# The context tiles' first layer half moved from a stage of its own into the 32 experts before it

## The reference

```python
def expert_block(args):                       # first block, per expert
    xb, e = args
    gt = xb @ w_gate[e] + b_gate[e]
    up = xb @ w_up[e] + b_up[e]
    gt = jnp.minimum(gt, SWIGLU_LIMIT)
    up = jnp.clip(up, -SWIGLU_LIMIT, SWIGLU_LIMIT)
    hdn = gt * jax.nn.sigmoid(SWIGLU_ALPHA * gt) * (up + 1.0)
    return hdn @ w_down[e] + b_down[e]
...
def chunk_mlp(h, n_chunks, w_in, norm_g, norm_b, w_s, b_s, w_out):
    z = jax.nn.gelu(h @ w_in)
    u, v = jnp.split(z, 2, axis=-1)
    v = layer_norm_2(v, norm_g, norm_b)
    vb = v.reshape(bsz, n_chunks, CHUNK, A_HEADS, A_GROUP)
    s = jnp.einsum('hpq,bnqhc->bnphc', w_s, vb) + b_s.T[None, None, :, :, None]
    return (u * s.reshape(bsz, t, A_WIDTH)) @ w_out
...
def one_block(xb):                            # peer_ffn, 8 heads, 128 + 128 sub-keys
    q = (xb @ w_q).reshape(PEER_BLOCK, PEER_HEADS, 2, PEER_HALF)
    s = jnp.einsum('thpd,pkd->thpk', q, sub_keys).astype(jnp.float32)
    # top 16 of either half, top 16 of the 256 sums, softmax
    act = jax.nn.gelu(jnp.einsum('thkd,td->thk', u_tab[idx], xb)) * wts
    return jnp.einsum('thk,thkd->td', act, v_tab[idx])
...
# second block, layer 0: x are the 256 latent tokens (the first block's output), ctx 256 given ones
h_lat = x * (1.0 + s1) + sh1
mix_lat = chunk_mlp(h_lat, lat_chunks, *prm)
mix_ctx = chunk_mlp(ctx * (1.0 + s1c) + sh1c, ctx_chunks, *prm)
x = layer_norm_2(DN_ALPHA * x + g1 * mix_lat, ln_g[i, 0], ln_b[i, 0])
ffn_lat = peer_ffn(x * (1.0 + s2) + sh2, ...)
ctx = layer_norm_2(DN_ALPHA * ctx + g1c * mix_ctx, ln_g[i, 0], ln_b[i, 0])
ffn_ctx = peer_ffn(ctx * (1.0 + s2c) + sh2c, ...)
```

## Time and profile before

| what | us |
|---|---|
| three runs | 3847.1, 3851.69, 3853.88 (median 3851.69) |
| the profiled execution | 3846.67 |
| its span, from the first to the last instruction | 3844.9 |
| PE busy | 3362.8 (87%) |
| DVE busy | 1772.8 (46%) |
| ACT busy | 1112.3 (29%) |
| POOL busy | 855.5 (22%) |
| mean rate of the DMA engines | 359 GB/s |

### The profile page before, as it was taken

How to read it: one execution, slowest core, us unless ns; L and a number is a source line. 1 busy time by engine, 2 the same in 40 slices (tenths; PEclk the granted TensorE clock), 3 DMA queues, 4 the chain that set the end, 5 groups by cost and what they waited for, 6 DMA issues and landing times. The chain is left out here.

```text
span 3844.9 us, 36626 instructions
## 1 busy us (share of the span) xinstructions
PE 3362.8 (87%) x11836; PEld 1520.8 (40%) x11836; DVE 1772.8 (46%) x4114; ACT 1112.3 (29%) x2981; POOL 855.5 (22%) x796
## 2 busy tenths in 40 slices
PE   8988999999999988788979779898887987877876
PEld 7635444444444435333335324343323543322322
DVE  0152211111111133576676686668753256767665
ACT  0141011111111111343343344544333213434333
POOL 0010000000000000334444344344440004444442
PEclk9999799999999989899999999999999988999999
DMA  6496699999999942999999999999996109999998
GB/s 277 162 387 245 252 423 423 423 423 420 423 423 423 421 174 94 368 421 422 422 417 415 419 406 398 422 421 398 422 421 276 58 28 397 421 421 421 407 421 335
DMA packets 157485, 1379.45 MB, mean 359 GB/s; under 512 B 18521, under 2 KB 19161, under 8 KB 25634
## 3 DMA queue, kind: packets, MB, share of 16 engines
q0 software_dynamic: 111360, 805.46, 50.6%
q1 hardware_dynamic: 45986, 572.36, 36.3%
HBM read 1376.59 MB, written 1.15 MB: 358 GB/s over the span
## 5 line engine op out<-in xcount | busy, mean ns | idle before, releaser
L2378 PE MATMUL ps<-sb_arena,sb_diag 128*128 128x512 f32 x3072 | 1486.8, 623 | 349.6 <-ACT sb_diag L2358 348.1
L2289 POOL DMA_INDIRECT sb_arena<-in_uv,sb_idx x768 | 842.8, 1097 | 2666.0 <-POOLq L1470 1247.8
L2317 DVE SCALAR_TENSOR_TENSOR sb_arena<-sb_arena,sb_H 128x1024 f32<-128x1024 f32 x768 | 940.8, 1226 | 633.5 <-DMA sb_arena<-in_uv,sb_idx 474.4
L2378 PEld LDWEIGHTS ps<-sb_arena,sb_diag 128*128 128x128 f32 x3072 | 561.7, 195 | 1231.6 <-ACT sb_diag L2358 670.4
L962 PE MATMUL ps<-sb_ring,sb_arena 128*64 128x512 f32 x3072 | 682.6, 597 | 0.0
L2349 ACT ACTIVATE sb_act<-sb_dots 128x1 f32<-128x1 f32 x768 | 154.9, 202 | 1099.3 <-DVE sb_arena L2317 1097.2
L962 PEld LDWEIGHTS ps<-sb_ring,sb_arena 128*64 128x64 f32 x3072 | 212.7, 137 | 442.0 <-issue 438.1
L2358 ACT ACTIVATE sb_diag<-sb_consts,sb_act 128x128 f32<-128x128 f32 x768 | 308.4, 402 | 25.6 <-PE ps L2378 0.6
L1096 DVE TENSOR_SCALAR sb_arena<-ps 128x512 f32<-128x512 f32 x32 | 22.1, 692 | 554.4 <-PE ps L962 554.4
L2353 ACT ACTIVATE sb_act<-sb_act,sb_wts 128x1 f32<-128x1 f32 x768 | 226.2, 295 | 24.9
L171 PE MATMUL ps<-sb_ring,sb_arena 128*128 128x512 f32 x480 | 211.1, 599 | 5.7 <-PE ps L171 1.5
(11 more groups left out here) (296 smaller groups left out, 2281.0 us busy)
## 6 DMA issues: line engine op xcount, KB each, us to landing
sb_ring<-in_moe SPq DMA_DIRECT2D x192, 2048.0 KB, 10.2
sb_ring<-in_w_mod SPq DMA_DIRECT2D x24, 2048.0 KB, 9.4
sb_ring<-in_w_in SPq DMA_DIRECT2D x11, 2048.0 KB, 13.8
sb_ring<-in_a_w_in SPq DMA_DIRECT2D x8, 2048.0 KB, 11.2
sb_ring<-in_b_w_in SPq DMA_DIRECT2D x8, 2048.0 KB, 12.3
sb_ring<-in_w_q SPq DMA_DIRECT2D x6, 2048.0 KB, 12.1
sb_arena<-in_uv,sb_idx POOLq DMA_INDIRECT x768, 15.2
sb_ring<-in_a_w_out SPq DMA_DIRECT2D x4, 2048.0 KB, 10.9
```

The costliest lines, as they stand in the source:

```text
L2289: pool.indirect_dma_start(uv[n_ % BUFS], None, table, bass.IndirectOffsetOnAxis(m.idx[:, pair % 2, k:k + 1], 0))\
L2317: nc.vector.scalar_tensor_tensor(out=u, in0=u, scalar=1.0, in1=m.H[:, order[i], :], op0=ALU.mult, op1=ALU.mult, accum_out=m.dots[:, n_ % P ...
L2378: last = nc.tensor.matmul(out[h], m.diag[n_ % DIAGS], uv[b][:, D + h * 512:D + (h + 1) * 512], start=opens, stop=ends)
```

## The change

The stage between experts and gathers is taken apart. A new class `Context` holds all of the context tiles' work up to the first search. It is written as generators that yield expert numbers, and in each expert PE issues what is due behind the turned weights and ahead of the down products, ACT behind its copy of the turned weights, DVE at the expert's end. For that the loop over experts is written out 32 times on every engine (the loop stays for the overflow). The pieces on PE: transposes in experts 1, 2, 13, 14, 20 and 22; products with weight chunks in 3, 5, 8, 11 (MLP in), 15, 17 (MLP out), 23, 25 (queries); mixing in 9 and 10; scores in 26 to 29. They alternate between banks 7 and 5.

The eight context chunks stand in the ring ahead of the down chunks of those experts. From expert 26 on the ring uses five slots, since the context's scores lie in slot 0. `retire` goes; semaphores are cleared by SP inside the next block. `ctx_mlp` and `ctx_scores` are gone. The latent tiles' opening is the first part of `Late`, in the first slots of `peer` (the pieces' pace is 1.3, counted from -12), and SP loads its rows and the first two side chunks at the end of `moe`. The last scatter closes the sums, without zero products.

```diff
+LASTING = ("mod_out", "bank_", "chunk_", "dve_step", "rows_in", "variance_ready", "std_ready", "consts_in",
+           "late_", "side_", "search_step", "peer_", "wts_ready", "idx_ready")
+CONTEXT_AT = {3: 0, 5: 1, 8: 2, 11: 3, 15: 4, 17: 5, 23: 6, 25: 7}
+FIVE_FROM = 26
...
+class Context:
...
+        self.plan = banks.plan(names, [7, 5])
...
+    def wait_left(self, pe, bank):
+
+        if bank in self.sent:
+            pe.wait_ge(self.M(f"bank_free{bank}"), self.sent[bank][1] + 1)
...
+        def open_bank(where, e):
+            banks.wait_free(pe, where)
+            if where[0] == 7:
+                pe.wait_ge(M("xe_ready"), e + 2)
+            else:
+                pe.wait_ge(M("u_ready"), e + 1)
+            self.sent[where[0]] = where
...
+        def wide(where, t, chunk, e):
+            w = self.ring.wait(pe, f"context{chunk}")
+            open_bank(where, e)
+            banks.fill(products(nc, m.ps[:, where[0], :], [(hT[:, k, t * P:(t + 1) * P], w[:, k, :]) for k in range(KT)]), where)
...
+        for n, e in enumerate((3, 5, 8)):
+            yield e
+            pe.wait_ge(M("context_hT"), 2 * TT)
+            for t in range(TT):
+                wide(plan["z", n, t], t, n, e)
...
+            def expert(p, e):
...
+                        if c == 2:
+                            context.wait_left(pe, 5)
...
+                context.wait_left(pe, 7)
+                gather(p, picked(p, e, 2))
...
+                last.then_inc(M(name("weigh_turned", p)), 1)
+                if p == 0:
+                    beside.upto(e)
+
+                pe.wait_ge(M(name("hT_ready", p)), at(p, e, 1))
+                for c in (4, 5):
...
+                if p == 0:
+                    for e in range(NE):
+                        expert(p, e)
+                else:
+                    with pe.Fori(0, NE) as e:
+                        expert(p, e)
...
-            scatter()
-            for i in range(4):
-                last = nc.tensor.matmul(acc[i], m.const("zero"), x.xe.rearrange("p a b -> p (a b)"), start=False, stop=True, skip_group_check=True)
-            last.then_inc(M("sums_done"), 1)
+            scatter(True).then_inc(M("sums_done"), 1)
...
-LATE_PACE = 1.4
+LATE_PACE = 1.3
...
+    def open(self, step):
+
+        for t in range(TT):
+            x = self.m.X[:, t, :]
+            step(self.nc.vector.scalar_tensor_tensor(out=x, in0=x, scalar=ALPHA1, in1=self.m.ps[:, 2 * t:2 * t + 2, :].rearrange("p a b -> p (a b)"),
+                                                     op0=ALU.mult, op1=ALU.add), "late_opened")
...
+            yield from norm(x, self.opening + t + 1, at["open", t] + 1)
+            for i, (dst, src, op) in enumerate(((x, x, ALU.mult), (x, x, ALU.add), (H[:, t, :], x, ALU.mult))):
+                yield at["open", t] + 7
...
+        for e in range(NE):
+            for c in range(PER_EXPERT):
+                if c == 4 and e in CONTEXT_AT:
+                    front.append((f"context{CONTEXT_AT[e]}", context[CONTEXT_AT[e]], SLOT))
+                front.append((f"moe{e}.{c}", d["moe"][e, c], SLOT))
+        six = sum(1 for name, _, _ in front if not name.startswith("moe") or int(name[3:].split(".")[0]) < FIVE_FROM)
+        chunks = [(*chunk, n % NSLOT) for n, chunk in enumerate(front[:six])]
+        chunks += [(*chunk, 1 + n % (NSLOT - 1)) for n, chunk in enumerate(front[six:])]
```

826 lines of the change are left out of this document (481 added, 345 removed).

## The result

| | us |
|---|---|
| before, four runs beside the changed kernel | 3851.07 (3847.1 to 3853.88) |
| the changed kernel, four runs | 3804.52 (3798.59 to 3807.28) |
| ratio | 0.9878, 95% interval 0.9861 to 0.9895 |
| its profiled execution, span | 3807.14, 3805.3 |
| forecast | 3819.5, range 3806 to 3844 |

The profiled executions differ by 39.6 us (span 3844.9 and 3805.3). The same kernel in a later set had 3808.14, which lies inside the range: whether the median falls just in or just out of it is within what two sets of runs differ by.

What follows compares the result with a forecast made beforehand. PE sets the pace in the experts, the DMA bounds the first search, so earlier gathers shorten the end. 39.3 - 2.1 - 2 - 0 - 3 = 32 us off the 3851.7 us median gives 3819.5; range 3806 to 3844.

Steps and rivals of the forecast that it cites:

- rival: Five: everything hides (0.58 with forecast), DVE-bound search front 0.13, pieces delay experts 0.10, written-out experts slower 0.10, comes out even 0.06.
- signs that it named for being right: PE never idle in experts, 29.79 us apart without a piece; first gather some 39 us earlier, DMA engines full from there.
- those for being wrong: PE waits for chunks after expert 26 or banks; experts' stage grows over 128 us; first to last gather over 1353 us.
- End of the experts: Last down product to first gather: 12.8 us instead of 180.4, 167.6 us less.
- What PE takes over: Context products moved into the experts, where PE has no idle time, cost their full time: 128.3 us.
- Waits inside the experts: Waits for copies, DVE or the five-slot ring from expert 26 on: 2 us taken, bounds 0 and 18.
- written-out experts: Experts' loop written out 32 times costs nothing: 0 us taken, bounds 0 and 64 us.
- What the DMA takes over: Latent tiles' loads after the last down product leave 2.1 us of older traffic before the first gather: cost 2.1 us.
- the opening: Latent tiles' residual, normalization and modulation in the search's first slots; DVE lumps idle the DMA: 3 us, bounds 0 and 10.
- From profile to median: Whole kernel: profiled 3814.5 us after; the median lies 5.0 us above the profiled execution, so 3819.5.

Runs made afterwards that it cites:

- e3: The changed kernel with the first context chunk's products (expert 3, two tiles, 32 records) done twice: 3820.09 us, ratio 0.9931.
- e1: The kernel before with two broadcast rows loaded at the start of the experts' stage instead of ahead of the router's weights: 3844.74 us, ratio 0.9992.
- e2: The kernel before with the loops over experts written out 32 times on PE, ACT, DVE and SP: 3850.95 us, ratio 1.0008.
- e5: The changed kernel with a ring of five slots from expert 4 on instead of from expert 26 on: 3806.82 us, ratio 0.9885.
- e8: The changed kernel with the latent tiles' first two weight chunks loaded at the start of the peer block, not behind the last down chunk: 3816.17 us, ratio 0.9912.
- e4: The changed kernel with the last multiplication of each latent tile's opening written five times instead of once, for larger DVE lumps: 3812.13 us, ratio 0.9905.
- e7: The changed kernel with two broadcast rows (1 MB) loaded in addition ahead of the router's weights: 3810.38 us.

## Why the prediction was wrong

The mechanism was right where the prediction looked, and no rival took its place: PE sets the pace of the experts, the old stage had room that PE did not use, and the search behind follows the first gather. The signs that it named for being right came, but for the first gather, which is 44 us ahead of the old one and not 39, and none of those for being wrong did. What failed is a stage at which it did not look, and some sizes. The steps in turn:

- **End of the experts**, 167.6: measured 167.0. Right.
- **What PE takes over**, 128.3: the stage grew by 125.9. Right in kind (e3), 2.4 too large. The rows of the context's 20 pieces do add up to 128.3 in the changed kernel, but from the start of each to the start of the next row it is 126.9, because a row of PE ends up to 0.07 us after the next has begun (531.29 + 13.90 = 545.19 against 545.12): rows that touch must not be added by their durations. The other 1.0 is as much as the experts of the kernel before differ by (956.1 in e1, 957.2 in e2).
- **Waits inside the experts**, 2, and **written-out experts**, 0: both 0 (e5, e2). The 2 had no row behind it; the prediction itself said that every row shows slack.
- **What the DMA takes over**, 2.1, and **the opening**, 3: together first to last gather grew by 2.2, not 5.1. (Profiles of unchanged code there have 1348.1, 1350.6 and 1350.0 us, and the five of the new 1349.5 to 1352.8, so the growth is known to some 2 us only.) The older traffic is 3.0 to 3.8 us (e8), where 2.1 were forecast. The single lumps left the DMA engines' share full, and the rate lacks at most 0.8 us, where 3 were forecast; that price was argued from gathers "emptied", and e4 shows that what comes on top of such lumps is paid nearly whole. Against that, the window behind the first gather, in which four loads of half a MB used to be issued, had lacked 1.6 us before and lacks nothing now; the sum did not have this.
- **The missing term.** The sum began at the experts. The prediction counted the four rows where they arrive, behind the last down product, and put nothing for the place that two of them left, ahead of the router's weights in `route`. e1 and e7 put 4 us on it: PE's wait for the router's inputs fell from 5.25 to 1.04 us. This is the step that failed.
- **From profile to median.** The forecast took the median 5.0 us above the profiled execution, as the shown runs had it. After the change the median of the set was 2.6 below its profile. That makes 7.6 of the 15.0 us by which the forecast missed; the other 7.4 are the sum. In the second set profile and median were 3808.06 and 3808.14, and the 21 runs of the kernel before in that set have a median of 3848.57, 3.1 below that of the three shown runs: such an offset between one execution and a median of three is chance, and does not carry over. By the same chance the miss of the range could have been a hit.

Taken as measured, the sum in the profile is 167.0 - 125.9 - 2.2, and 2.9 at the start, less 2.7 and plus 0.4 behind the search: 39.6 (before rounding), where the terms of the forecast add to 32.2. Of the 7.4 that it lacked, 4.2 are the router's wait, 2.4 PE's products, 2 the waits, and 3 the front of the search; against them stand 1.3 (attention), 0.6 (end of the experts) and 2.3 behind the search, where the work is the same and the granted clock was 0.92 before and 0.90 after.

Two readings of the prediction are off without harm to the sum. The rows at 1321.56 and 1351.35 are the bias of up, not of gate; the period is the same 29.79 us. And 4719 records in 924.7 us against 2629 in 1298.1 are 2.5 times as dense, not twice.

## What to carry to other kernels

Price a moved DMA twice, once where it arrives and once where it leaves: 1 MB ahead of a stage's first input was worth 4 us, a tenth of the gain, in a stage that the change never spoke of. When an engine with idle time in one stage and none in the next is given work, the full price in the busy stage is the right term, from start to start of the rows, and allowances without a row behind them only spoil the sum. Where the DMA engines are the bound, look for the windows in which they are idle (here 16 us at 6 GB/s, just ahead of the stage that they bound): filling it was worth 4 to 5 us. Look at the share beside the rate, too: a window at a lower rate and a full share is not one of idle engines.

## What the runs showed of the hardware

The granted clock decides some microseconds per execution and is not the change's doing. The stage between the two searches has the same work in all kernels, but took from 268.6 to 276.8 us between the last gather of layer 0 and the first of layer 1. Its windows in the kernel with the two rows moved (e1) and with five slots (e5):

```profile
2903.61:3172.19 268.58, 223.76 (x807) 121.69 (x806) 107.27 (x229) 59.30 (x107) 0.00 (x1) 0.93 0.26 99
```

```profile
2862.89:3139.69 276.80, 232.28 (x807) 125.27 (x806) 107.25 (x229) 59.27 (x107) 0.00 (x0) 0.90 0.25 96
```

The same 807 records of PE take 223.8 us at a mean clock of 0.93 and 232.3 at 0.90, while DVE's time is equal to 0.02 us. This alone is as large as most terms above, and is the reason that they were read in stretches of the profile and not from medians.

The DMA engines move 420 to 423 GB/s in most of the full windows of 10 to 25 us shown here. The two windows below that at the same share of 1.01, 388 and 405 GB/s, have 1070 of 1625 and 582 of 1350 packets under 8 KB; the first window of the changed kernel's search, with 385 of 1177, still moves 421. The Trainium skill ("Perfetto Trace Analysis", Roofline) bounds a single core by its 16 DMA engines at about 435 GB/s; the windows at 422 lie 3% below that.
